# Differential-attention encoder layer on one core: all gate panels behind the head loop, and one projection unit between two score blocks

## The reference

```
u = rmsnorm(h, norm_g[0])
proj = u @ w_in                                   # (1024 x 1024) @ (1024 x 5120)
hc, bc, cc, q, k, v, gates = split(proj)
y_conv = (bc * conv3(cc * hc)) @ w_conv_out       # short gated convolution, 3 taps
a = softmax(q1 k1' * scale + bias) - lam * softmax(q2 k2' * scale + bias)
o = rmsnorm(a @ v, subln_g) * (1 - lam_init)      # 4 heads; bias is ALiBi
y_attn = o @ w_attn_out
g = sigmoid(gates + b_gate)                       # two branches of 1024 channels
m = (g[0] * y_conv + g[1] * y_attn) @ w_o
h = h + rmsnorm(m, norm_g[1])
u = rmsnorm(h, norm_g[2])
out = h + rmsnorm(square(relu(u @ w_ff1)) @ w_ff2, norm_g[3])
```

## Time and profile before

| | us |
|---|---|
| median of 3 runs | 1436.82 |
| lowest, highest | 1436.71, 1437.62 |
| the profiled execution | 1436.46 |
| its span | 1434.7 |
| TensorE busy | 1394.5 |
| VectorE busy | 924.4 |
| ScalarE busy | 567.0 |

### The profile page before, as it was taken

One profiled execution on the slowest core, in us unless ns is written; L12 is line 12 of the kernel. 1 busy time (PEld: TensorE's weight loads), 2 busy tenths in 40 slices (PEclk: granted clock), 3 DMA queues, 4 the chain that ended last, 5 costly groups with the idle time before them and its releaser, 6 DMA issues.

```text
span 1434.7 us, 17064 instructions
## 1 busy us (share of the span) xinstructions
PE 1394.5 (97%) x6281; PEld 1131.5 (79%) x6281; DVE 924.4 (64%) x1306; ACT 567.0 (40%) x871; POOL 111.3 (8%) x73
## 2 busy tenths in 40 slices
PE   5999999999999999999999999999999999999997
PEld 4877778777787777878788877888888877888886
DVE  6485576757657664156555698667774677775576
ACT  5434443533434454211233344333332444454453
POOL 0000000000000000000000143323333100000000
PEclk9999999999999999999999999999999999999999
DMA  5211111111111112344542155444444955336333
GB/s 166 59 30 59 42 33 60 44 29 44 58 29 29 58 66 74 103 154 143 192 165 72 44 169 161 143 152 161 161 147 148 387 199 170 102 97 226 95 111 132
DMA packets 141463, 161.96 MB, mean 113 GB/s; under 512 B 6813, under 2 KB 88922, under 8 KB 141274
## 3 DMA queue, kind: packets, MB, share of 16 engines
q1 hardware_dynamic: 135392, 148.40, 32.1%
q10 hardware_dynamic: 6010, 12.75, 2.3%
HBM read 114.98 MB, written 46.14 MB: 112 GB/s over the span
## 4 chain that ended last, share of the span: by engine, by line
PE 76%; DVE 10%; ACT 5%; issue 5%; DMA 4%; SPq 0%; ACTq 0%; DVEq 0%
PE psum L711 40%; PE psum L890 17%; PE psum L951 12%; DMA f_raw<-f_scratch 3%; PE psum L781 2%; PE psum L766 1%; PE psum L879 1%; DVE op L1749 1%; DVE v L1769 1%; PE psum L770 1%; DVE t_sum L1665 1%; DVE op L1752 1%; DVE v L1876 1%; ACT op L1253 1%; ACT w_hi L993 1%
## 5 line engine op out<-in xcount | busy, mean ns | idle before, releaser
L951 PE MATMUL psum<-op 128*128 128x512 f32 x1344 | 307.7, 390 | 2.9 <-DVE op L1752 2.6
L951 PEld LDWEIGHTS psum<-op 128*128 128x128 f32 x1344 | 251.4, 188 | 59.0 <-issue 4.4
L711 PE MATMUL psum<-act_hi,w_hi 128*128 128x512 f32 x640 | 257.8, 403 | 2.6 <-ACT staging L1059 2.3
L711 PE MATMUL psum<-act_hi,w_lo 128*128 128x512 f32 x640 | 250.4, 391 | 0.0
L711 PE MATMUL psum<-act_lo,w_hi 128*128 128x512 f32 x640 | 250.0, 391 | 0.0
L711 PEld LDWEIGHTS psum<-act_hi,w_hi 128*128 128x128 f32 x640 | 120.6, 188 | 31.7 <-issue 8.3
L711 PEld LDWEIGHTS psum<-act_hi,w_lo 128*128 128x128 f32 x640 | 120.5, 188 | 25.8
L711 PEld LDWEIGHTS psum<-act_lo,w_hi 128*128 128x128 f32 x640 | 120.8, 189 | 25.4 <-issue 1.9
L1749 DVE TENSOR_TENSOR op<-v,op 128x512 fp32r<-128x512 f32 x112 | 78.3, 699 | 71.1 <-ACT op L1253 71.1
L1396 DVE TENSOR_TENSOR w_lo<-w_raw,w_hi 128x1024 fp32r<-128x1024 f32 x52 | 65.1, 1252 | 82.0 <-ACT w_hi L993 80.2
L1253 ACT ACTIVATE op<-v 128x512 fp32r<-128x512 f32 x112 | 70.4, 628 | 118.2 <-DVE v L1769 69.1
(11 more groups left out here) (218 smaller groups left out, 2470.2 us busy)
## 6 DMA issues: line engine op xcount, KB each, us to landing
f_raw<-f_scratch SPq DMA_DIRECT2D x112, 256.0 KB, 2.7
w_raw<-in_w_in SPq DMA_DIRECT2D x40, 512.0 KB
w_raw<-in_w_ff SPq DMA_DIRECT2D x32, 512.0 KB, 4.9
f_scratch<-f_out SPq DMA_DIRECT2D x56, 256.0 KB, 2.3
gates_scratch<-staging ACTq DMA_DIRECT2D x32, 256.0 KB, 2.0
gate_in<-gates_scratch SPq DMA_DIRECT2D x16, 512.0 KB, 4.2
v<-in_w_ff SPq DMA_DIRECT2D x8, 1024.0 KB, 7.9
v<-in_w_ff SPq DMA_DIRECT2D x4, 2048.0 KB, 10.4
```

Of the source, the lines that this page charges most:

```text
L711: mm = nc.tensor.matmul(bank, stat(a, kt), moving(b, kt), start=(n == 0), stop=(n == len(terms) - 1))
L951: mm = nc.tensor.matmul(psum[:, (X_BANK, Z_BANK)[m % 2][t]], op[n % SLOTS][:, 2 + a, token_cols(t)], op[n % SLOTS][:, b], start=(m in (0, ...
```

## The change

`TURN` is written anew. The four gate units g0 to g3 leave it; `HEAD_PANELS` falls from 8 to 6, and the plain gate turns, `Fori(HEADS + len(AFTER), HEADS + GATE_TURNS)`, grow from 2 to 6. The remaining units stand one by one between the score blocks: v0 no longer ahead of S0 but behind it, v1 behind T0, h0 with VT0 behind T1, and so on to b1 behind T6. Each T stands directly behind the next block's S. The taps are a step of their own, K0, ahead of b0. `vt` lies in the gates' staging buffer, not in e[1]; the waits and the counts follow. VectorE's set-up of the table, which stood before v0 in turn 0, now stands before S0; on VectorE both places are the same, behind k1.

```diff
-TURN = steps("C7 q0 O0 q1 T7 TL7 k0 AV1 k1 v0 O1 v1 S0 VT0 h0 X0 M0 C0 h1 S1 X1 T0 M1 TL0 C1 c0 S2 X2 T1 M2 "
-             "TL1 C2 c1 S3 X3 b0 T2 M3 TL2 C3 b1 S4 X4 g0 T3 M4 TL3 C4 g1 AV0 S5 X5 T4 M5 TL4 C5 g2 S6 X6 T5 "
-             "M6 TL5 C6 g3 S7 X7 T6 M7 TL6")
+TURN = steps("C7 q0 O0 q1 T7 TL7 k0 AV1 k1 O1 S0 X0 v0 M0 C0 S1 X1 T0 M1 TL0 C1 v1 S2 X2 T1 M2 TL1 C2 h0 VT0 S3 X3 T2 M3 TL2 "
+             "C3 h1 S4 X4 T3 M4 TL3 C4 c0 AV0 S5 X5 T4 M5 TL4 C5 c1 S6 X6 T5 M6 TL5 C6 K0 b0 S7 X7 T6 M7 TL6 b1")
+V_TURN = len([x for x in TURN[:TURN.index(("VT", 0))] if x[0] == "T" and x[1] < 7])
...
-HEAD_PANELS = len(PANELS) - 1 + GATE_PANELS
+HEAD_PANELS = len(PANELS) - 1
...
+        vt = junk
...
-                    vt = e[1]
...
-                columns += [i * GATE_PANELS + (COL_G // P + g) for g in range(GATE_PANELS)]
...
-            with sp.Fori(HEADS, GATE_TURNS) as i:
+            with sp.Fori(0, GATE_TURNS) as i:
...
-                            wait(pe, gate_ready, i * GATE_UNITS - (1 - h))
+                            wait(pe, z_ready, i * 2 - (1 - h))
...
-                        elif n < 2 and not after:
-                            pe.wait_ge(z_ready, i * 2 + (1 + h))
+                        elif n < 2 and isinstance(i, int) and i == HEADS:
+                            pe.wait_ge(z_ready, HEADS * 2 - (1 - h))
                         else:
-                            pe.wait_ge(gate_ready, i * GATE_UNITS + (n - 1))
+                            pe.wait_ge(gate_ready, (i - HEADS) * GATE_UNITS + (n - 1))
...
-            with pe.Fori(HEADS + len(AFTER), GATE_TURNS) as i:
+            with pe.Fori(HEADS + len(AFTER), HEADS + GATE_TURNS) as i:
...
-                            wait(act, a_ready, i * QB)
+                            if not (isinstance(i, int) and i == 0):
+                                act.wait_ge(tb_done, tb_use(i - 1, "VT", 0) + 1)
...
+                            if n == 0 and isinstance(i, int) and i == HEADS:
+                                act.wait_ge(tb_done, tb_use(HEADS - 1, "VT", 0) + 1)
                             if n == 0:
-                                act.wait_ge(bias_ready, i + 1)
-
-                            wait(act, gate_stored[h], i * (16 * GATE_PANELS) + 16 * (n // 2))
+                                act.wait_ge(bias_ready, i - HEADS + 1)
...
-                            if h == 1:
-
-                                for tap in range(CONV_K):
-                                    wc = par[:, bass.ds(i + (PAR_C + tap * CT), 1)]
-                                    win = inner[:, tap:tap + S]
-                                    if tap == 0:
-                                        dve.wait_ge(c_ready, i * 2 + 2)
-                                        vec.tensor_scalar(one(z, i), win, wc, None, ALU.mult).then_inc(taps, 1)
-                                    else:
-                                        dve.wait_ge(taps, i * CONV_K + tap)
-                                        vec.scalar_tensor_tensor(out=one(z, i), in0=win, scalar=wc, in1=one(z, i),
-                                                                 op0=ALU.mult, op1=ALU.add).then_inc(taps, 1)
...
-                        if (kind, n) == (("g", 0) if after else ("c", 0)):
-                            wait(dve, gate_ready, i * GATE_UNITS)
-                            vec.tensor_scalar(gate_bias[:], par[:, bass.ds(i * GATE_PANELS + PAR_B, GATE_PANELS)], 0.5,
-                                              None, ALU.mult).then_inc(bias_ready, 1)
+                        if (kind, n) == ("g", 0):
+                            wait(dve, gate_ready, (i - HEADS) * GATE_UNITS)
+                            vec.tensor_scalar(gate_bias[:], par[:, bass.ds((i - HEADS) * GATE_PANELS + PAR_B, GATE_PANELS)],
+                                              0.5, None, ALU.mult).then_inc(bias_ready, 1)
...
+                    elif kind == "K":
+                        for tap in range(CONV_K):
+                            wc = par[:, bass.ds(i + (PAR_C + tap * CT), 1)]
+                            win = inner[:, tap:tap + S]
+                            if tap == 0:
+                                dve.wait_ge(c_ready, i * 2 + 2)
+                                vec.tensor_scalar(one(z, i), win, wc, None, ALU.mult).then_inc(taps, 1)
+                            else:
+                                dve.wait_ge(taps, i * CONV_K + tap)
+                                vec.scalar_tensor_tensor(out=one(z, i), in0=win, scalar=wc, in1=one(z, i),
+                                                         op0=ALU.mult, op1=ALU.add).then_inc(taps, 1)
...
-                        dve.wait_ge(tb_hi, i * (QB + 1) + {"VT": 1, "TL": 2 + n if n < 7 else 0}[kind])
+                        dve.wait_ge(tb_hi, i * (QB + 1) + {"VT": V_TURN + 1, "TL": n + 1 + (n >= V_TURN) if n < 7 else 0}[kind])
...
-            first = FIRST_TURN.index(("v", 0))
+            first = FIRST_TURN.index(("S", 0))
```

More of the change, by code:

```diff
@@ L159, in unit_of @@
     if after:
-        return i * (2 * GATE_PANELS) + (2 * HEADS * (len(PANELS) - 1) + n)
+        return (i - HEADS) * (2 * GATE_PANELS) + (HEADS * HEAD_UNITS + n)
     return i * HEAD_UNITS + (2 * PANELS.index(kind) + n)
 def panel_of(i, kind, n, after=False, ahead=0):
-    per, first = (GATE_PANELS, HEADS * (len(PANELS) - 1)) if after else (HEAD_PANELS, PANELS.index(kind))
+    per, first = (GATE_PANELS, HEADS * (HEAD_PANELS - GATE_PANELS)) if after else (HEAD_PANELS, PANELS.index(kind))
     j = first + n // 2 + ahead
@@ L1053, in walk @@
                         elif kind == "g":
+                            if n == 0 and isinstance(i, int) and i == HEADS:
+                                act.wait_ge(tb_done, tb_use(HEADS - 1, "VT", 0) + 1)
                             if n == 0:
-                                act.wait_ge(bias_ready, i + 1)
-                            wait(act, gate_stored[h], i * (16 * GATE_PANELS) + 16 * (n // 2))
+                                act.wait_ge(bias_ready, i - HEADS + 1)
+                            wait(act, gate_stored[h], (i - HEADS) * (16 * GATE_PANELS) + 16 * (n // 2))
                             nc.scalar.activation(staging[h][:], psum[:, h], ACT.Tanh, scale=0.5,
                                                  bias=gate_bias[:, n // 2:n // 2 + 1]).then_inc(gate_ready, 1)
-                            act.wait_ge(gate_ready, i * GATE_UNITS + (n + 1))
-                            act.dma_start(one(gates.rearrange("b k p s -> p (b k) s"), i * GATE_PANELS + n // 2)
+                            act.wait_ge(gate_ready, (i - HEADS) * GATE_UNITS + (n + 1))
+                            act.dma_start(one(gates.rearrange("b k p s -> p (b k) s"), (i - HEADS) * GATE_PANELS + n // 2)
                                           [:, half_cols[h]], staging[h][:]).then_inc(gate_stored[h], 16)
@@ L1100, in _ @@
             nc.scalar.preload_act_table(ACT.Tanh)
-            with act.Fori(HEADS + len(AFTER), GATE_TURNS) as i:
+            with act.Fori(HEADS + len(AFTER), HEADS + GATE_TURNS) as i:
                 walk(i, [("g", n) for n in range(GATE_UNITS)], True)
@@ L1568, in _ @@
                 walk(HEADS + n, steps, True)
-            with dve.Fori(HEADS + len(AFTER), GATE_TURNS) as i:
+            with dve.Fori(HEADS + len(AFTER), HEADS + GATE_TURNS) as i:
                 walk(i, [("g", n) for n in range(GATE_UNITS)], True)
```

## The result

The changed kernel takes 1466.84 us (median of 4 runs, 1466.05 to 1467.37) against 1436.82: a ratio of 1.0207, with an interval of 1.019 to 1.0225. It is 30 us slower. The forecast was 1476.8 with a range of 1465 to 1486. The sign and the place were right, the size was 10 us too large; the measured time lies 1.8 us above the lower end of the range.

The account below looks back on a forecast made before the run. TensorE, busy 97%, was taken to set the time. Stalls and half clock of 11.4 us in head 0 and 32.85 in heads 1 to 3, less gains of 4.4, made +39.9: a median of 1476.8, range 1465 to 1486.

Parts of the forecast that it names:

- term 1: S0 behind k1: S0 waits for k's low part, TensorE idles 3.6 us a turn, 4.1 in head 0.
- term 2: First block, heads 1 to 3: S1 waits 1.9 us for M0's read, T0 2.55 for the combination.
- Term 3: Later blocks: v's low part delays T2 by 0.9 us, c1's multiply and split T6 by 0.4; 1.3 a turn.
- Term 4: Clock: half rate behind the idles at S0 (hidden in S1's wait in heads 1 to 3) and T0; 1.6 us a turn.
- The turn of 111.2: Forecast length in us of one head turn in the changed kernel, against 123.25 before.
- gains of 4.4: Savings in us: 3.2 from old waits at T and O0 going, 1.2 from fewer slower unit starts.
- The signs: Expected profile: S0 waits 3.6 to 4.1 us four times, S1 up to 2; two half-clock stretches a turn; gate loop without waits.
- (a): Rival: the same stalls in the head turns with the clock full, +31.9 us, 1468.8; chance 0.2.
- (b): Rival: dips at every gap and of double length, or blocks slipping at more places; +8 us, 1484.8; chance 0.15.
- (c): Rival: the shorter head turn stays covered at S0, only the gains are left, 1432.4; chance 0.03 together with (d).
- (d): Rival: gate units still needed in the heads, so they merely move and no stall shows; chance 0.03 with (c).

Follow-up runs that it names:

- Experiment 2: Kernel before with its gate units kept in the head turns, but S0 directly behind k1 and O1 and the other units spread over the blocks; 1454.35 us, ratio 1.0125.
- experiment 3: Changed kernel with O1's reciprocal and scaling moved behind c0 and the table's rescaling ahead of k0, emptying VectorE's queue before X0; 1474.49 us.
- experiment 5: Changed kernel with v0 behind M0 in the list, so ScalarE takes M0's exponential before v0's copy, TensorE's order the same; 1463.86 us.
- experiment 6: Changed kernel with v0 behind M0 for ScalarE, the table's rescaling ahead of k0 and O1's reciprocal between TL3 and C4; 1456.82 us.
- experiment 4: Changed kernel with 14 extra matmuls, their result unread, in TensorE's idle time ahead of S0; 1465.71 us.
- experiment 7: The kernel of experiment 6 with AV1 moved between k1 and S0, and O1 behind S0; 1442.0 us.
- experiment 1: Changed kernel with its gate panels behind the heads, but the other units back in the order of the kernel before; 1503.54 us, ratio 1.047.

## Why the prediction was right, and what was too large

- **Terms 1 and 2 held.** From k1's end to T0 the forecast was 17.6 us and the turns have 17.7. Experiment 2 shows term 1 alone, experiments 3, 5 and 6 term 2: M0's exponential had two holds, VectorE's queue and v0's copy, that ended almost together (M0's read at 13.3 and v0's copy at 13.75 in the working), and each alone was worth little. In head 0 the half clock lasted longer than taken (52.37 to 59.30 at 0.58, 2.9 us lost instead of 1.6), and T0 came at 18.5 instead of 17.6.
- **Term 3** was 0.9 + 0.4 a turn and measured 0.78 + 0.21, at the places named (T2 behind v's low part, T6).
- **Term 4 failed.** "The idle of 2.55 at T0 does it again" is the step that was wrong: the idle came (2.58 to 2.79), and the clock stayed at 1.00 in all four turns. That is 6.4 of the 10 us. Only one execution was profiled, but the other three have mean clocks of 0.992 to 0.994 against its 0.991, so they spent no more time at half clock. Why the clock stayed full there is open. At S0 the clock fell in all four turns, as the forecast had it, and experiment 4 shows that this loss is hidden in turns 1 to 3. Another 3.3 us (1.55 in the gate stage, and 1.76 between 701.88 and 863.85 before, 732.36 and 892.57 now) stood in no term: the two half-clock stretches that the kernel before has outside the heads, behind idles of 2.27 and 2.01 us, didn't come in the changed kernel, though the idles did (500.23 and 732.36).
- **The reckoning.** The forecast difference of 39.9, less 6.4 (T0's clock), 3.3 (the two stretches), 1.2 (term 3) and 0.6 (0.2 in each of three turns that these terms leave, not traced further), plus 0.95 (head 0) and 0.3 (0.1 in three turns), is 29.65. The spans differ by 29.6. The fit is close in part by construction, since the 0.6 is a rest; the start of the kernel (0.8 shorter to head 0's k1) and its end (0.9 longer behind 892.57) cancel. The turn of 111.2 takes off 1.2 where a quarter of the gains of 4.4 is 1.1; it measured 109.2.
- **The signs.** S0's wait came four times, but the list shows 3.05 us in turns 1 to 3 where 3.6 to 4.1 was named: it counts from the modelled end of O1's matmuls (267.58 + 1.02), while S0 starts where the forecast had it. S1's wait for M0's read isn't in the list, and each turn has one half-clock stretch behind k1, not two. The gate loop runs at 5.44 us a unit, and its waits of 2.27 and 1.09 at its two ends are in the kernel before, too (2.27 and 1.05).
- **The gains** of 3.2 at T and O0 came: no wait of O0 is left, and none at T1. The table load stands directly behind O1's square root (271.85) and costs nothing, as worked out from the earlier trace rows.
- **The rivals.** (a), the stalls with a full clock, gave 1468.8 and was nearest, with half its reason: the clock was full behind T0, not behind S0. That it came within 2 us is partly luck, since the 3.3 us outside the heads stood in none of its terms either. (b) fell: no block slipped beyond T2 and T6, and only head 0's half clock was longer than taken. (c) and (d) fell with the first row of the waits.
- **The Trainium skill's warning** ("TensorE: Matmul & The Clock Gate", "Why this matters for your kernels") is about longer gaps than the 2.6 to 2.8 us at T0, so the prediction went beyond it in setting a dip beside every new gap. In the change the clock fell behind the gaps at S0 (3.05 to 3.9 us), four of four, and behind none of the four at T0, which agrees with the page. Over all runs it also fell behind 13 of 38 gaps of 2.0 to 2.95 us (the table below), which that section doesn't name.

## What to carry to other kernels

Before filler work is moved away from a chain of dependent steps, write down for each wait what the gap would be without it: the number of units a turn mattered little here (25 of 30 us came back with the same number), their places and those of the dependent steps nearly all. Where a result has just been made (k's low part, 4 us through two engines), its reader must not be next in the order; put a step there that is ready, even one moved from elsewhere (AV1). And an operation with two holds, one in each of two queues, shows little gain until both are gone (in turns 1 to 3 T0's 2.6 us fell by 0.35 at most); look in every engine's list for what stands between a result and its reader.

## What the runs showed of the hardware

The half clock behind an idle stretch of TensorE isn't a fixed price. The table has each idle stretch of TensorE of 1.5 us or more between 25 and 1200 us in the ten profiles; the clock is the mean granted clock of the 3.4 us behind it:

| idle, us | stretches | with the clock below 0.8 behind them |
|---|---|---|
| 3.9 to 4.6 | 20 | 20 |
| 3.05 | 15 | 12 |
| 2.8 to 2.95 | 9 | 6 |
| 2.5 to 2.6 | 7 | 2 |
| 2.24 to 2.27 | 12 | 3 |
| 2.0 | 10 | 2 |
| 1.6 to 1.75 | 11 | 3 |

The same wait at the same place fell either way in different kernels: behind 2.27 us in the gate stage the clock was half in the kernel before, in experiments 6 and 7, and full in the change. All three cases in the last row are S7 in experiment 1, 1.1 us of matmuls behind the wait of 2.85 us at T5. One half clock costs about 1.6 us (the gate stage from that wait to its end lasts 57.3 us before, and 142.8 in the change with 16 units of 5.44 more, 1.55 less than the sum). Two windows of the change, behind S0 and behind T0:

```profile
271.65:275.20 3.55, 3.54 (x12) 2.25 (x13) 3.55 (x2) 1.47 (x2) 0.00 (x0) 0.72 0.25 73
285.27:288.67 3.40, 3.40 (x19) 2.98 (x20) 2.84 (x8) 1.90 (x3) 0.00 (x0) 1.00 0.00 0
```

What decides it between 1.6 and 3.1 us of idle stays open. An estimate: at 1.6 us each, one to four stretches that fall in one kernel and not in the other are 2 to 6 us of a comparison of two orders, as much as small edits are worth. So a small edit is better judged by the wait that it was to remove than by the time alone.
